# Moving the first convolution taps and the gelu of a seven-product tile later in the ScalarE and VectorE queues of a ConvFFN

## The reference

```python
def _conv_ffn(h, prev, w_gate, w_up, conv_w, conv_b, w_down):
    t = h.shape[1]
    gate_in = h @ w_gate
    buf = jnp.concatenate([prev.astype(gate_in.dtype), gate_in], axis=1)
    conv = conv_b
    for j in range(CONV_W):
        conv = conv + conv_w[j] * buf[:, j:j + t]
    out = (jax.nn.gelu(conv) * (h @ w_up)) @ w_down
    return out, buf[:, -(CONV_W - 1):]
```

## Time and profile before

| | |
|---|---|
| median of three runs | 843.82 us |
| the profiled execution: its own time | 844.54 us |
| its span, first to last instruction | 842.7 us |
| mean granted TensorE clock | 0.994 |
| TensorE busy (PE / PEld) | 96% / 91% |
| VectorE busy | 63% |
| ScalarE busy | 46% |
| GpSimd busy | 23% |

### The profile page before, as it was taken

How to read it: one execution, slowest core, us unless ns; L and a number is a source line. 1 busy time by engine, 2 the same in 40 slices (tenths; PEclk the granted TensorE clock), 3 DMA queues, 4 the chain that set the end, 5 groups by cost and what they waited for, 6 DMA issues and landing times.

```text
span 842.7 us, 16965 instructions
## 1 busy us (share of the span) xinstructions
PE 809.1 (96%) x7218; PEld 766.3 (91%) x7218; DVE 527.1 (63%) x826; ACT 383.6 (46%) x589; POOL 192.0 (23%) x151
## 2 busy tenths in 40 slices
PE   5999999998999999999999999999999999999995
PEld 5898998787989999985599999999999999999995
DVE  6699999797358535114236988888888869210113
ACT  7544415757646325123324745454555558222221
POOL 1000002010640341430044220202020224844430
PEclk9999999999999999999999999999999999999998
DMA  9151204445555494329213222323332342433303
GB/s 337 57 148 51 76 26 152 155 122 169 163 183 158 131 415 140 91 86 412 87 51 100 76 76 101 100 102 100 101 101 101 101 145 81 127 100 103 104 1 102
DMA packets 33597, 106.03 MB, mean 126 GB/s; under 512 B 4186, under 2 KB 9306, under 8 KB 31090
## 3 DMA queue, kind: packets, MB, share of 16 engines
q1 hardware_dynamic: 33522, 104.95, 37.3%
HBM read 96.28 MB, written 6.71 MB: 122 GB/s over the span
## 4 chain that ended last, share of the span: by engine, by line
PE 67%; DVE 20%; ACT 7%; DMA 3%; issue 3%; SPq 1%; DVEq 0%; ACTq 0%
PE pj L711 13%; PE pj L713 13%; PE pj L712 13%; DMA w_raw<-in 3%; PE aux L718 3%; PE aux L720 3%; PE aux L719 3%; PE pj L718 2%; PE pj L720 2%; PE pj L719 2%; DVE w_lo L1941 2%; PE aux L1262 2%; PE pj L1332 2%; DVE h_lo L1932 1%; PE pj L1039 1%
## 5 line engine op out<-in xcount | busy, mean ns | idle before, releaser
L679 POOL TENSOR_TENSOR w_lo<-w_raw,w_hi 128x512 fp32r<-128x512 f32 x100 | 137.7, 1399 | 479.7 <-ACT w_hi L1476 479.6
L711 PE MATMUL pj<-h_hi,w_hi 128*128 128x260 f32 x720 | 206.0, 286 | 12.2 <-DVE w_lo L1988 9.0
L713 PE MATMUL pj<-h_hi,w_lo 128*128 128x260 f32 x720 | 204.3, 284 | 0.0
L712 PE MATMUL pj<-h_lo,w_hi 128*128 128x260 f32 x672 | 190.5, 283 | 0.0
L1476 ACT ACTIVATE w_hi<-w_raw 128x1024 fp32r<-128x1024 f32 x77 | 81.4, 1057 | 165.2 <-PE pj L713 134.9
L711 PEld LDWEIGHTS pj<-h_hi,w_hi 128*128 128x128 f32 x720 | 136.6, 190 | 14.9 <-DVE w_lo L1988 9.0
L713 PEld LDWEIGHTS pj<-h_hi,w_lo 128*128 128x128 f32 x720 | 136.6, 190 | 0.0
L712 PEld LDWEIGHTS pj<-h_lo,w_hi 128*128 128x128 f32 x672 | 127.5, 190 | 0.0
L679 POOL TENSOR_TENSOR wx_lo<-w_raw,wx_hi 128x512 fp32r<-128x512 f32 x36 | 48.2, 1369 | 102.7 <-ACT wx_hi L1476 102.7
L2623 DVE TENSOR_TENSOR conv<-pj,rinv 128x520 f32<-128x520 f32 x7 | 4.9, 699 | 79.7 <-PE pj L713 79.7
L711 PE MATMUL pj<-h_hi,wx_hi 128*128 128x260 f32 x176 | 49.9, 283 | 0.8 <-DVE h_lo L1932 0.8
(11 more groups left out here) (487 smaller groups left out, 2319.0 us busy)
## 6 DMA issues: line engine op xcount, KB each, us to landing
w_raw<-in SPq DMA_DIRECT2D x126, 512.0 KB, 3.7
caches<-in SPq DMA_DIRECT2D x14, 1024.0 KB, 11.6
vpg<-in SPq DMA_DIRECT2D x16, 256.0 KB, 3.1
kpg<-in SPq DMA_DIRECT2D x12, 256.0 KB, 3.1
x<-in SPq DMA_DIRECT2D x4, 520.0 KB, 7.3
out<-x SPq DMA_DIRECT2D x16, 130.0 KB, 1.9
out<-kT SPq DMA_DIRECT2D x1, 1040.0 KB
u<-kT SPq DMA_DIRECT2D x16, 64.0 KB, 2.0
```

The costliest lines, as they stand in the source:

```text
L679: nc.gpsimd.tensor_tensor(lo[:, part], w_raw[:, raw_of(n) % 4, part], hi[:, part].bitcast(F32), ALU.subtract).then_inc(lo_done, 1)
L711: pe.matmul(out, s_hi, m_hi_, start=first, stop=False)
L712: pe.matmul(out, s_hi, m_lo_, start=False, stop=False)
L713: ins = pe.matmul(out, s_lo, m_hi_, start=False, stop=last)
```

## The change

In the loop over the seven-product tiles of a group, `last_tap(t)` and `first_taps(t)` are no longer issued at the end of tile t's own turn but inside the next tile's turn: on ScalarE behind the next tile's first copy, on VectorE behind its corner read. The gelu, `ff_open(t - 1)`, moves from ahead of the next weight's high part to behind the second copy. Nothing is added or taken away.

```diff
                 for t in run:
                     copy_chain(t, 0)
                     if t > run[0]:
+                        last_tap(t - 1)
                         high_seven(t, 3)
-                        ff_open(t - 1)
                     if t < run[-1]:
                         high_seven(t + 1, 0)
                     else:
                         high(UNIT[t + 1])
                     copy_chain(t, 1)
+                    if t > run[0]:
+                        ff_open(t - 1)
                     copy_chain(t, 2)
                     if t < run[-1]:
                         high_seven(t + 1, 1)
                         high_seven(t + 1, 2)
-                        last_tap(t)
                     else:
                         high(UNIT[t + 1] + 1)
...
                 for t in run:
                     read_first(t)
                     if t > run[0]:
+                        first_taps(t - 1)
                         low_seven(t, 3)
...
                     read_last(t)
                     if t < run[-1]:
                         low_seven(t + 1, 2)
-                        first_taps(t)
```

## The result

| | before | changed |
|---|---|---|
| median, runs of one chip | 844.0 us (841.81 to 845.44, 12 runs) | 846.37 us (843.81 to 849.85, 12 runs) |
| ratio, 95% interval | | 1.0029 [1.0015, 1.0043] |
| the profiled execution's span | 842.7 us | 845.4 us |
| mean granted TensorE clock | 0.994 | 0.995 |

The changed kernel is slower by 0.3%, some 2.4 us (1.3 to 3.6 by the interval), where +0.6 was forecast, and 846.37 lies just above the range.

A forecast was written before the change was run, and what follows sets the result against it. TensorE was taken to bound the kernel, only its waits winnable. Per group 0.53 + 0.52 - 0.79 = +0.26, in four +1.05; last pair and tail -0.47; sum +0.6 on the median 843.82 gives 844.4, range 842.2 to 846.2.

The forecast's parts named there:

- stall two: Third tile of each full group: VectorE and GpSimd meet, `read_mid` is late, product 7 waits 0.52 us, bounds 0 and 1.1.
- the last pair: Tiles 19 and 20 with the tail to 709 us: stall +0.19, `a_lo` wait falling from 0.70 to 0.04, -0.47 us.
- What the change removes: Third tiles of the full groups: all eight waits before products 3 and 5 go, 0.79 us a group.
- Stall one: Middle tile: taps behind the corner read delay `read_mid`, so product 7 waits 0.53 us, bounds 0.4 and 0.6.
- `read_mid(5)` needs its `a_made`: Tile 5: multiplication ends at 531.89, `read_mid` runs 531.92 to 532.35, product 7 may load at 532.46.
- Rival 2: Third tiles and last pair: GpSimd and VectorE block each other for whole lengths, +3.3 us, 847.1; chance 0.05.
- If VectorE comes first: Tile 20 near 692 us: L2551 precedes GpSimd's fourth half, `gate` 0.47 earlier, `a_lo` wait falls to 0.04.
- rival 1: Tile 20: GpSimd first at 692 us, last pair and tail +0.63, total +1.7, 845.5; chance 0.27.
- its own row of 490.60 and 490.61: Profile rows near 490 us where GpSimd won a near-tie with VectorE, cited for GpSimd coming first at 692 us.
- Rival 3: Third tile: half low part goes before GpSimd, `read_mid` ends in time, -1.6 us, 842.2; chance 0.08.
- rival 4: Middle and third tiles: VectorE has room, both product 7 stalls absent, -3.7 us, 840.1; chance 0.03.
- The late loads for tile 7: SyncE's next two weight loads, delayed 2.2 us by the late half low part, costed at nothing.

The follow-up runs named there:

- The gelu alone: Kernel before with only the gelu moved behind the next tile's second copy, all taps staying: 843.35 us against 844.21, ratio 0.9993; a second look 843.87 us.
- `read_mid` first: Changed kernel with `read_mid` ahead of the next tile's corner sums in the middle tiles: 846.81 us, ratio 1.004.
- GpSimd's MEMSET: Changed kernel with GpSimd writing zeros instead of the low parts of plain tiles 6, 10, 14, 18, 21: 843.43 us, ratio 0.9985.
- the high part later: Changed kernel with the next plain tile's first high part behind the third copy in the third tile, releasing GpSimd later: 845.92 us against 844.4, ratio 1.0021.
- the faster version: Kernel before, last tap behind the first copy only in each group's last tile, gelu behind the second copy in middle and last tiles: 842.51 us, ratio 0.9974.

## Why the prediction was wrong

Its mechanism in the groups came as it was worked out, and so did the sign there; the size of stall two and the last pair did not. The stretch grew by 2.3 us where 0.57 was worked out, so 1.7 are missing: 0.6 in stall two, 1.15 in the last pair, less 0.1, because the waits that go are 0.81 a group on the average and not the 0.79 of tile 5.

**What the change removes: right.** All eight waits before products 3 and 5 are gone. The gelu alone takes those before product 5 away. One reading on the way was wrong and cost nothing: the low part that ended at 525.8 is `u+2`, which product 5 needs; product 3's `u+1` had been done at 523.59, two microseconds before. The changed kernel shows it. VectorE and the weight load of product 3 in tile 5:

```profile
526.10 1.22 DVE L2528 TENSOR_TENSOR wx_lo<-w_sum,wx_hi 128x1024 fp32r<-128x1024 f32 x1
```

```profile
526.60 0.19 PEld L718 LDWEIGHTS aux<-f_hi,w_hi 128*128 128x128 f32 x1
```

That low part ends at 527.32, and product 3 has begun at 526.60 with no wait. So the first copy alone made it late before.

**Stall one, 0.53 us: right.** `read_mid(4)` ends at 522.16, and product 7 starts 0.11 later, 0.52 late. The experiment with `read_mid` first agrees with the cause, VectorE's full queue: the wait went from there and came back, larger, in the third tile.

**Stall two, 0.52 us: right in kind, mis-sized.** The changed trace runs 0.42 us later than that of before already at the middle tile's corner read (516.32 against 515.90), as at the start of the stretch. With that added, the forecast puts GpSimd's start at 528.71, the end of the half low part at 530.89 and of the second multiplication at 532.31. The rows show 528.70, 530.89 and 532.33. The alternation read from the earlier trace rows is thus right to 0.02 us over five steps. What failed is the step behind it, "`read_mid(5)` needs its `a_made`: 531.92 to 532.35". I gave it 0.03 after the multiplication's end, and it takes 0.13 to 0.14 in all five third tiles of the changed kernel, tile 20 among them, and in both tiles with `read_mid` first, one of them with the multiplication not stretched. The wait measured 0.67 on the average; 0.15 in four groups is 0.6 us of the 1.7 that are missing. The missing release is 0.10 of each 0.15; the rest is small differences between the groups.

**The Trainium skill's rule.** "SBUF — State Buffer", section "Who interferes with whom", has the second of the two blocked until the first has finished. The runs agree on which pairs meet: the half low part and the second multiplication, both with two SBUF inputs, are stretched, and L2496 between them, with one operand in PSUM, keeps 0.42 us. GpSimd's MEMSET, which reads nothing, doesn't stretch the half low part; the multiplication met no MEMSET. By whole lengths the third tile's wait would be 1.1; it is 0.67. Rival 2 is out.

**The last pair, -0.47: wrong, and this is the larger error, 1.1 us.** The step that failed is "If VectorE comes first". GpSimd came first, rival 1. VectorE's and GpSimd's timelines at 694 us:

```profile
694.10 1.81 DVE L2552 TENSOR_TENSOR gate<-gate,rinv 128x520 f32<-128x520 f32 x1
```

```profile
L679 POOL TENSOR_TENSOR w_lo<-w_raw,w_hi x4: 1281/1607/1811, 689.2 to 694.1; 128x512 fp32r<-128x512 f32 x4
```

The fourth half (the last of the four, at 694.1 in the tile view of 689 to 696 us) and L2552 start within rounding of each other. L2552 takes 1.81 us, not the 1.17 of the earlier trace rows, and its 0.64 us pass through taps, gelu and `a_lo`. Last pair and tail give 0.36 + 1.02 - 0.70 = +0.68, where rival 1 had +0.63; the last pair put back as before gave 0.66 less. The forecast had the tie at 0.06 us and took the side that its own row of 490.60 and 490.61 spoke against.

A row of one tie was little to go by, though. The trace before has another in the same tile 20, which went the other way: the second multiplication keeps its usual 0.42 us, and GpSimd's half takes 1.56 and not 1.3.

```profile
687.12 1.56 POOL L679 TENSOR_TENSOR w_lo<-w_raw,w_hi 128x512 fp32r<-128x512 f32 x1 [25.63 <-ACT w_hi L1476]
```

```profile
687.12 0.42 DVE L2497 TENSOR_TENSOR a_raw<-acc,conv 128x260 f32<-128x260 f32 x1
```

Over the twelve traces, from 470 us on, 52 pairs with SBUF operands alone start within 0.05 us of each other. In 48 GpSimd kept its 1.3 us and VectorE was stretched, also where VectorE's start is the earlier by up to 0.02; in four it was the reverse. What decides them is not known. The chance for rival 1, 0.27, was too small.

**The range.** The measured 1.56 of the four groups and 0.68 of the last pair are 2.2 us, on the forecast's 843.8 that is 846.1. The range's end was 846.2. So the range had little left for the measurement itself: the interval of the ratio alone is worth 1.2 us each way. The chance for slower by over 0.2% was set at 0.19 for the same two reasons.

**The other rivals.** Rival 3 (no meeting) and rival 4 (VectorE has room) did not come; the experiment with the high part later makes rival 3's condition by hand, and it does take away the third tile's wait. The late loads for tile 7, costed at nothing, made no weight load wait in the changed kernel. In one trace of the gelu alone late loads did, ahead of tiles 15 and 19.

## What to carry to other kernels

When work is moved within an engine's queue, its wait can turn up at what is now behind it: count the idle time of that engine from the release it waits for to the next one it gives, and how early that one comes. Here it was 0.21 us of idle time, and 0.6 us by which `read_mid` came early, for 1.53 us of taps. Move only the instruction that stands in a late one's way, in the tile where it does, as the faster version does. When an engine off the critical path is set going earlier or later, look whom it meets, and treat starts less than 0.1 us apart as undecided. Here GpSimd, the dearer side, took nearly all the ties.

## What was not expected of the hardware

`read_mid`, where it waits for the instruction directly ahead of it on its own engine, started 0.14 us after that one's end, where an instruction without such a wait starts about 0.08 before it. The third tap, which also waits for the one ahead, starts 0.04 after it; `read_mid` waits for several events, but whether that is the reason was not tried. VectorE and GpSimd subtracting in SBUF gave each other turns: the half low part took 1.79 us for 0.68, four halves 6.01 us for the 5.04 of before, yet the same half low part beside GpSimd's MEMSET took 0.69. Of 512 KB loads into `w_raw` the one issued second near 613 us took 4.45 us from issue to landing before the change, and 6.64 and 5.21 in two executions of the gelu alone. The first weight load of the ConvFFN that waits for `h_lo` came at 469.49 to 473.31 us in twelve executions, so the times of single executions hide what their stretches show to 0.1 us.
